# Two edits in the first 30 microseconds of a two-layer encoder kernel: a weight's low part moved two steps earlier on VectorE, and 18 more matmuls of ones around the first spreading

## What is computed

```
h = rms_norm(x, norm_g[0, 0])          # x * rsqrt(mean(x*x) + eps) * g
proj = h @ w_in                        # q, k, v, r of the first layer
gate_pre = (h @ w_gate_a) @ w_gate_b + b_gate
...
x = x + rms_norm(o, norm_g[i, 1])
h = rms_norm(x, norm_g[i, 2])
x = x + rms_norm(squared_relu_mlp(h, w_up, w_down), norm_g[i, 3])
```

## Time and profile before

| | |
|---|---|
| time, median of 3 runs | 2576.3 us (2575.55 to 2576.51) |
| profiled execution, its own time | 2575.64 us |
| its span, first to last instruction | 2573.9 us |
| mean granted TensorE clock | 0.988 |
| busy: PE / DVE / ACT / POOL | 97% / 36% / 33% / 21% |
| instructions | 41,743 |

### The profile page before, as it was taken

How to read it: one execution, slowest core, us unless ns; L and a number is a source line. 1 busy time by engine, 2 the same in 40 slices (tenths; PEclk the granted TensorE clock), 3 DMA queues, 4 the chain that set the end, 5 groups by cost and what they waited for, 6 DMA issues and landing times.

```text
span 2573.9 us, 41743 instructions
## 1 busy us (share of the span) xinstructions
PE 2502.4 (97%) x17518; PEld 2370.1 (92%) x17518; DVE 922.4 (36%) x1813; ACT 838.3 (33%) x1658; POOL 542.6 (21%) x304
## 2 busy tenths in 40 slices
PE   8999999999999999999998999899999999999998
PEld 8888887799999999999998877699999999999997
DVE  6555545437221221221237244517312212212226
ACT  5554545446121121121126455536311211211112
POOL 0101010134221121121126111014311211211213
PEclk9999999999999999999999999899999999999999
DMA  3101101124111111111104100004211111111114
GB/s 109 50 10 48 34 24 40 34 87 130 47 45 41 49 41 41 49 41 41 61 31 154 54 26 18 30 34 141 68 42 50 41 41 49 41 41 49 41 53 135
DMA packets 62720, 138.98 MB, mean 54 GB/s; under 512 B 8544, under 2 KB 39520, under 8 KB 62592
## 3 DMA queue, kind: packets, MB, share of 16 engines
q1 hardware_dynamic: 54720, 130.51, 15.3%
q10 hardware_dynamic: 7808, 6.56, 0.9%
q0 software_dynamic: 64, 0.10, 0.0%
HBM read 117.74 MB, written 19.40 MB: 53 GB/s over the span
## 4 chain that ended last, share of the span: by engine, by line
PE 90%; DVE 5%; ACT 2%; issue 2%; ACTq 0%; POOL 0%; DMA 0%; SPq 0%; DVEq 0%; POOLq 0%
PE banks L223 53%; PE banks L203 24%; PE banks L1939 4%; PE banks L2093 1%; PE banks L2090 1%; PE banks L2074 1%; PE banks L1450 1%; PE banks L1431 1%; DVE y L650 1%; PE banks L1418 1%; DVE w_lo L174 1%; DVE norm_acc L599 1%; PE banks L2058 1%; PE banks L1458 0%; PE banks L408 0%
## 5 line engine op out<-in xcount | busy, mean ns | idle before, releaser
L166 POOL TENSOR_TENSOR w_lo<-w_raw,w_hi 128x1024 fp32r<-128x1024 f32 x164 | 404.5, 2470 | 1857.0 <-ACT w_hi L159 1857.0
L203 PE MATMUL banks<-h_hi,w_hi 128*128 128x384 f32 (+1 forms) x1224 | 428.1, 350 | 3.3 <-DVE h_lo L1708 2.2
L203 PE MATMUL banks<-h_lo,w_hi 128*128 128x384 f32 (+1 forms) x1224 | 406.5, 332 | 0.0
L203 PE MATMUL banks<-h_hi,w_lo 128*128 128x384 f32 (+1 forms) x1224 | 406.0, 332 | 0.0
L159 ACT CAST w_hi<-w_raw 128x1024 fp32r<-128x1024 f32 x180 | 187.1, 1046 | 467.8 <-DMA w_raw<-in_units 467.6
L223 PE MATMUL banks<-h_hi,w_hi 128*128 128x384 f32 (+1 forms) x1368 | 301.8, 329 | 0.0
L223 PE MATMUL banks<-h_lo,w_hi 128*128 128x384 f32 (+1 forms) x1368 | 301.4, 328 | 0.0
L223 PE MATMUL banks<-h_hi,w_lo 128*128 128x384 f32 (+1 forms) x1368 | 301.3, 328 | 0.0
L223 PE MATMUL banks<-mlp_a_hi,w_hi 128*128 128x384 f32 (+1 forms) x1344 | 297.6, 329 | 1.5 <-issue 1.3
L223 PE MATMUL banks<-mlp_a_lo,w_hi 128*128 128x384 f32 (+1 forms) x1344 | 296.1, 328 | 0.0
L223 PE MATMUL banks<-mlp_a_hi,w_lo 128*128 128x384 f32 (+1 forms) x1344 | 296.0, 328 | 0.0
(11 more groups left out here) (205 smaller groups left out, 3194.6 us busy)
## 6 DMA issues: line engine op xcount, KB each, us to landing
w_raw<-in_units SPq DMA_DIRECT2D x180, 512.0 KB, 3.5
x_scratch<-y SPq DMA_DIRECT2D x48, 192.0 KB, 2.6
norm_x<-x_scratch SPq DMA_DIRECT2D x28, 192.0 KB, 3.2
x_scratch<-y SPq DMA_DIRECT2D x24, 160.0 KB, 1.8
norm_x<-x_scratch SPq DMA_DIRECT2D x20, 160.0 KB, 2.9
y<-in_x SPq DMA_DIRECT2D x16, 192.0 KB, 4.8
out_y<-y SPq DMA_DIRECT2D x16, 192.0 KB, 3.2
norm_x<-in_x SPq DMA_DIRECT2D x12, 192.0 KB, 3.7
```

The costliest lines, as they stand in the source:

```text
L166: c.nc.gpsimd.tensor_tensor(c.w_lo[:, s], c.w_raw[:, s], c.w_hi[:, s].bitcast(F32), ALU.subtract).then_inc(self.ready, 1)
L203: mm = chip.nc.tensor.matmul(out, w, x, start=(first and n == 0), stop=(last and n == 2))
```

## The change

Two edits, both in the first layer's start. TensorE's 26 matmuls of ones stay; 8 more of the same are put between `sums` and `spread` of block 0, and 10 more between that `spread` and `start_together`. On VectorE, the low part of unit 0 is made ahead of step 0, directly behind the diagonals, instead of ahead of step 1. Units 1, 2 and 3 keep their places (the new expression gives unit 1 at s = 3 and unit 2 at s = 7).

```
-    PER_BLOCK, WARM_MATMULS = 3, 26
+    PER_BLOCK, WARM_MATMULS = 3, (26, 8, 10)
...
-        for _ in range(self.WARM_MATMULS):
-            nc.tensor.matmul(chip.banks[:, self.START_V_BANKS[0], 0:P], chip.ones[:], chip.ones[:], start=True, stop=True)
+        def keep_warm(n):
+
+            for _ in range(n):
+                nc.tensor.matmul(chip.banks[:, self.START_V_BANKS[0], 0:P], chip.ones[:], chip.ones[:], start=True, stop=True)
+
+        keep_warm(self.WARM_MATMULS[0])
         self.before.sums(pe, 0)
+        keep_warm(self.WARM_MATMULS[1])
         self.before.spread(pe, 0)
+        keep_warm(self.WARM_MATMULS[2])
         pe.wait_ge(self.rank_split, 1)
         start_together(0, 2)
...
         before.inverse(dve, 0)
         for s in range(KT + 1):
-            if s in (1, 3, 7):
-                chip.stream.first_low(dve, s // 2 if s < 7 else 2)
+            if s in (0, 3, 7):
+                chip.stream.first_low(dve, (s + 1) // 3 if s else 0)
             before.step(dve, 0, s)
         chip.stream.first_low(dve, 3)
```

## The result

The changed kernel takes 2583.43 us in the median of 11 runs (2581.28 to 2587.44); the kernel before, run beside it, 2576.51 us in the median of 11 (2574.85 to 2582.04). The ratio is 1.0023 with a 95% interval of 1.0014 to 1.0031. The change makes the kernel slower, by about 6 us by that ratio (the medians lie 6.9 apart). The forecast was 2574.9 us.

The account below looks back on a forecast made before the run. Until 39.74 us VectorE's list, not TensorE (97% busy), was taken to bound the start. +0.29 - 0.66 - 1.13 + 0.14 = -1.36 us, from the median 2576.3, gave 2574.9 us, range 2573.9 to 2577.6.

Parts of the forecast that it names:

- The step that failed: Behind TensorE's third values: the order of events stays the old one, moved 1.36 us earlier, with nothing tied to fixed times.
- rival E: Far behind the start: a gain or loss beyond 0.2% (5.2 us), needing a changed order of waits; chance 0.04.
- the prediction's own sign: First layer's start: forecast wrong if the third values don't come 1.4 us earlier, or do and the end doesn't.
- the forecast -1.36: Sum on VectorE's list: low part of tile 0 starts at 14.80 us instead of 16.16, and the total falls by 1.36.
- The eight matmuls: Ahead of block 0's spreading: they outlast the gap (+0.29 us) but hold the clock at 2.4 GHz (-0.66); net -0.37.
- rival C: Near 12.5 us the clock falls all the same; the path gains only 0.70 us, giving 2575.6 us; chance 0.08.
- The low part: Unit 0's subtraction hides in VectorE's idle time before the first scaling: -1.13 us, +0.14 for ScalarE's rounding; -0.99.
- The ten matmuls: Behind block 0's spreading: they end at 15.48 us, just ahead of TensorE's first real matmul at 15.50; cost 0.
- TensorE's own gain: Values of block 0 begin 2.8 us earlier, but waiting on VectorE's list lets no more than 1.36 us pass on.
- The wait for tile 2: TensorE, done with tiles 0 and 1 at 17.2 us, waits a new 1.4 us while VectorE makes unit 1's low part.
- Rival B: The clock falls at block 1's spreading after a 2.2 us wait, losing 1.7 or 3.4 us: 2576.6 or 2578.3; chance 0.33.
- the farther case: Half-rate stretch of 6.7 us behind the second spreading: 3.4 us lost, 2578.3 us, mostly left out of the range.

Follow-up runs that it names:

- after: The changed kernel (both edits) in its first profiled execution, against the kernel before: 2581.62 us; median of its 11 runs 2583.43 us.
- after_again: The full change once more, unchanged, against the kernel before on another chip: 2581.98 us, ratio 1.0018.
- ones_only: Only the 8 and 10 matmuls of ones added to the kernel before, low part left ahead of step 1: 2581.77 us, ratio 1.0015.
- after_four_fourteen: The full change with 26, 4 and 14 matmuls of ones instead of 26, 8 and 10, against the kernel before: 2580.94 us, ratio 1.0017.
- the padded kernel: The kernel before plus 72 TensorE instructions that compute nothing (waits already reached), no matmul added, low part not moved: 2578.9 us, ratio 1.0006.
- before: The kernel before, without either edit, in its profiled execution: 2575.64 us.
- low_only: Only the low part of unit 0 moved, no matmul added, against the kernel before: 2576.58 us, ratio 0.9997.
- low_eight: Low part moved and the eight matmuls ahead of the spreading, without the ten, against the kernel before: 2579.11 us, ratio 1.0005.
- low_ten: Low part moved and the ten matmuls behind the spreading, without the eight, against the kernel before: 2576.82 us, ratio 0.9995.
- same_length: The full change with 8, 8 and 10 matmuls of ones, as many instructions as the kernel before, measured against it: 2580.98 us, ratio 1.0014.
- after_pad_64: The full change plus 64 more TensorE instructions (waits already reached) around the second spreading, against the kernel before: 2578.24 us, ratio 1.0.
- after_stores_later: The full change with ScalarE's five cache stores two query tiles later, against the kernel before: 2576.99 us, ratio 1.0.
- before_look: The kernel before, unchanged, one further execution; the two times given there for the kernel before are 2577.7 and 2577.37 us.
- pad_72_look_c: The kernel before plus 72 TensorE instructions that compute nothing, one execution, its fourth look: 2582.33 us.
- low_stores_apart: Low part moved, no matmul added, and the five stores issued in five separate steps, against the kernel before: 2571.84 us, ratio 0.9981.
- before_stores_later: The kernel before with only ScalarE's five cache stores two query tiles later, against the kernel before: 2575.74 us, ratio 0.9992.

## Why the prediction was wrong, point by point

- **The price of 18 more matmuls was counted at the place where they run, and nowhere else.** The step that failed reads "from there on the order of events is the old one, moved: weights are loaded as slots come free, so nothing later is tied to a fixed time", and with it rival E, "Nothing in the trace reaches 5.2 us". By the prediction's own sign the start failed as well: the third values came 0.46 us later, not 1.36 earlier. Of the 7.2 us between the forecast -1.36 and the +5.9 of the profile, 2.7 arise at the start, 4.0 at the stores and 0.6 at other half-rate stretches. Code packets are tied to the count of instructions and not to the work. All eight profiled executions of kernels with 72 more instructions and the stores in their old place (after, after_again, ones_only, after_four_fourteen, and the padded kernel four times) have a stretched store, 1.28 to 2.11 us; of the seven with the code packet elsewhere (before twice, low_only, low_eight, low_ten, same_length, after_pad_64) none has. From the stores to 1490 us the lag, matmul by matmul, grows by 3.3 to 4.0 us in the six of the eight with 10.2 us of half rate behind the stores, by 0.7 and 1.0 in the two with 3.4, and by no more than 0.01 in the others, all against the kernel before. Against after_again's +4.7, taking the packet away saved 3.6 us (after_pad_64) and taking the stores away 4.8, of which the move itself is worth 1.5 (after_stores_later and its control). That the packet's arrival is the cause is shown by that; how it holds up a store's issue inside the DMA hardware is not.
- **The size of that loss varies from execution to execution.** In the profile of the changed kernel it is 1.5 us of stretch and 2.5 more for the half rate behind it. With padding alone it came to 1.8 us in the median with an interval from -1.0 to +4.1. The half rate that follows lasted 3.4 us in some executions and 10.2 in others, which is a scatter of some 3 us; the exact median stays unexplained.
- **The eight matmuls (+0.29 and -0.66): wrong in most executions.** I took -0.37 "since TensorE would be busy up to the moment at which it fell". Of the six profiles of kernels with 26 matmuls ahead of the sums and eight behind them, the clock fell ahead of the eight or within them in five (after, ones_only, low_eight, after_pad_64, after_stores_later) and held in one (after_again). At half rate they hold the spreading back, to 0.9 to 1.8 us behind the diagonals in these five. My rival C had the fall, but let the eight run at full rate, so its -0.70 was mis-sized too: the term that it priced at +0.29 measured +1.4.
- **The low part (-0.99): right in kind and nearly in size.** 0.91 us on VectorE's list in low_only; the gain in total time, 1.5 us, has an interval that holds 0.
- **The ten matmuls (0): right.** low_ten is no slower than low_only within their scatter (2576.82 against 2576.58), though its ten ran at half rate (3.85 us). TensorE's slack ahead of the sums of block 1 took them up, as argued.
- **TensorE's own gain passes on only as far as VectorE's list: right.** The wait for tile 2 was 0.98 us (1.4 forecast) and the one ahead of the second spreading 1.82 (2.2 forecast).
- **Rival B, the clock at the second spreading: it happened** in after, after_again, ones_only, after_four_fourteen, low_ten, same_length and after_pad_64, between 37.2 and 41.9 us, and cost 0.84 us in the profile after. It isn't the change's alone: before_look, the kernel before, has it too, at 40.3. The lengths that I gave half-rate stretches, 3.4 or 6.7 us, were misread: the trace of the kernel before has 10.2 too, at its very start (12.5 to 22.7), so the farther case was priced too low. The Trainium skill, page "TensorE: Matmul & The Clock Gate", part 1, has the gate decide at moments that run free of the kernel's start. The traces agree: the first fall came at 12.5, 11.4, 11.2, 11.9 and 10.8 us in five executions (before, after, low_only, low_eight, low_ten) whose sums began between 9.5 and 9.9.
- **Noise.** I took 0.7 us as the scatter, from three runs. Over three sets of 33 to 35 runs the kernel before spreads from 2574.15 to 2583.52. The slower of them have the lower mean granted clock: in the last set the median is 2574.6 at 0.989 (4 runs) and 2580.8 at 0.986 (6 runs).

## What to carry to other kernels

Instructions that compute nothing still have two prices: they run at the clock of their moment, and they shift every later fetch of code on their engine. When a change moves the time by more than its place can explain, compare the durations of DMA issues and the packets of the instruction queue at far places, and undo the shift with padding before blaming the work. A row of DMA issues on an engine that the critical path waits for is fragile; the kernel here that issues them one by one between other work, and moves the low part, is 5.4 us below the kernel before.

## What the hardware showed that was not expected

- A code packet of 16 KB on TensorE's queue among the 1,104 packets of ScalarE's stores stretched one store's issue from 0.64 to between 1.28 and 2.11 us in eight of eight executions. The Trainium skill, page "Trainium Kernel Development and Optimization", section "Key Constraints", says that DMAs issued from the SP, ACT and POOL queues share the same 16 engines and interleave. It doesn't speak of code packets; the row of 1472.00:1473.00 shows one on these engines beside ScalarE's stores.
- The clock fell at 11.38 us in the changed kernel although TensorE had had no idle time in the record since 9.71: by then it had done the twelve one-column records of the sums and begun on the matmuls of ones. What of it made the clock fall, no run here shows.
- A wait of 3.67 us rather than 2.20 was followed by 10.2 us at half rate rather than 3.4. The length of the wait alone doesn't decide: after 2.84 us (after_four_fourteen) it was 10.2, after 3.19 us (pad_72_look_c) it was 3.4.
- Five stores issued in a row cost the kernel before 3.6 us even without a code packet: that much comes back at this place when they are issued one by one (low_stores_apart) or moved away (before_stores_later).
